# Inverse of the RWKV chunk matrices: the transposed 32x32 blocks by a block transpose on VectorE instead of a third product on TensorE, and the cover pages dealt out anew

## The reference

```python
def step(S, inp):
    r_t, w_t, k_t, v_t, kk_t, a_t = inp
    sa = jnp.einsum('bhij,bhj->bhi', S, -kk_t)
    S = (S * w_t[:, :, None, :]
         + sa[..., None] * (kk_t * a_t)[:, :, None, :]
         + v_t[..., None] * k_t[:, :, None, :])
    y_t = jnp.einsum('bhij,bhj->bhi', S, r_t)
    return S, y_t
```

## Time and profile before

| what | value |
|---|---|
| median of 3 runs | 1367.03 us (1365.85 to 1368.22) |
| the profiled execution, its time | 1366.13 us |
| its span in the trace | 1364.3 us |
| TensorE busy over the span | 1269.6 us (93%) |
| VectorE, ScalarE, GpSimd busy | 811.6, 673.0, 569.9 us |
| chain that ended last | PE 58%, DMA 29%, ACT 5%, DVE 5%, issue 2% |

### The profile page before, as it was taken

The page is one execution under the profiler, slowest core; times in us unless marked ns, Lnnn a source line. Parts: engine busy times, 40 slices in busy tenths (PEclk is TensorE's granted clock), DMA queues, the critical chain, the costliest instruction groups (busy, mean ns, idle before and its releaser), DMA issues.

```text
span 1364.3 us, 22840 instructions
## 1 busy us (share of the span) xinstructions
PE 1269.6 (93%) x8934; PEld 910.7 (67%) x8934; DVE 811.6 (59%) x1854; ACT 673.0 (49%) x1501; POOL 569.9 (42%) x385
## 2 busy tenths in 40 slices
PE   9999999999999999999999988888889888888786
PEld 7988897989999999997896543333434333333232
DVE  5845202464568773457338776666677666667755
ACT  4710233646566665564325564454555444554544
POOL 1100023516878888740005444444434444444342
PEclk9999999999999999999999999999999999999999
DMA  7432322425645556557539999999999999999997
GB/s 265 140 100 90 110 90 75 131 93 171 200 158 188 181 186 200 157 163 267 222 105 414 420 421 422 422 421 421 421 422 422 422 421 421 421 422 422 422 422 302
DMA packets 67940, 381.10 MB, mean 279 GB/s; under 512 B 7552, under 2 KB 7552, under 8 KB 35200
## 3 DMA queue, kind: packets, MB, share of 16 engines
q0 software_dynamic: 37296, 268.45, 47.4%
q1 hardware_dynamic: 29664, 107.84, 24.1%
q10 hardware_dynamic: 880, 3.41, 0.7%
HBM read 378.63 MB, written 1.05 MB: 278 GB/s over the span
## 4 chain that ended last, share of the span: by engine, by line
PE 58%; DMA 29%; ACT 5%; DVE 5%; issue 2%; POOL 0%; SPq 0%; POOLq 0%; DVEq 0%; ACTq 0%
DMA arena_block<-in_experts,arena_block 28%; PE bank L467 23%; PE bank L1111 9%; PE bank L503 5%; PE bank L521 3%; PE bank L465 2%; DVE arena_block L2490 2%; PE bank L1035 2%; PE bank L908 2%; PE bank L485 1%; PE bank L566 1%; DMA const<-in_const 1%; ACT arena_block L1721 1%; PE bank L1135 1%; PE bank L1045 1%
## 5 line engine op out<-in xcount | busy, mean ns | idle before, releaser
L1111 PE MATMUL bank<-arena_block 128*128 128x512 f32 x1012 | 485.4, 610 | 83.4 <-ACT arena_block L1721 81.8
L2627 POOL DMA_INDIRECT arena_block<-in_experts,arena_block x253 | 272.6, 1077 | 467.5 <-PE bank L1111 330.6
L2490 DVE SCALAR_TENSOR_TENSOR arena_block<-arena_block 128x1024 f32<-128x1024 f32 x256 | 314.1, 1227 | 188.5 <-DMA arena_block<-in_experts,arena_block 184.4
L1111 PEld LDWEIGHTS bank<-arena_block 128*128 128x128 f32 x1012 | 178.1, 190 | 350.2 <-ACT arena_block L1721 212.6
L2604 POOL TENSOR_TENSOR w_lo<-ring,w_hi 128x1024 fp32r<-128x1024 f32 x100 | 242.8, 2449 | 85.0 <-ACT w_hi L1219 84.7
L1715 ACT ACTIVATE arena_block<-arena_block 128x1 f32<-128x1 f32 x256 | 75.1, 293 | 278.8 <-DVE arena_block L2490 278.5
L1219 ACT ACTIVATE w_hi<-ring 128x1024 fp32r<-128x1024 f32 x112 | 117.8, 1054 | 51.6 <-PE bank L503 28.8
L467 PE MATMUL bank<-x_hi,w_hi 128*128 128x256 f32 x384 | 109.0, 284 | 0.0
L467 PE MATMUL bank<-x_hi,w_lo 128*128 128x256 f32 x384 | 108.7, 283 | 0.0
L467 PE MATMUL bank<-x_lo,w_hi 128*128 128x256 f32 x384 | 108.7, 283 | 0.0
L1721 ACT ACTIVATE arena_block<-const,arena_block 128x128 f32<-128x128 f32 x256 | 102.7, 401 | 8.3
(11 more groups left out here) (538 smaller groups left out, 2344.6 us busy)
## 6 DMA issues: line engine op xcount, KB each, us to landing
ring<-in_pages SPq DMA_DIRECT2D x175, 512.0 KB, 3.5
wq_pages<-in_pages SPq DMA_DIRECT2D x16, 512.0 KB, 4.4
arena_block<-in_experts,arena_block POOLq DMA_INDIRECT x259, 14.9
arena_block<-in_pages SPq DMA_DIRECT2D x8, 512.0 KB, 7.0
arena_mix<-in_memT ACTq DMA_DIRECT2D x1, 1024.0 KB, 9.0
arena_block<-in_subkT ACTq DMA_DIRECT2D x1, 1024.0 KB, 5.4
const<-in_const SPq DMA_DIRECT2D x1, 974.5 KB, 13.3
out_tok<-arena_block SPq DMA_DIRECT2D x3, 256.0 KB, 7.6
```

What stands on the lines that cost most here:

```text
L1111: last = mm(bank[2 * tt + j][:, :], diag[:, slot, :], uv[slot][:, D + j * 512:D + (j + 1) * 512], start=start, stop=stop)
L2490: stt(uv[s][:, 0:D], uv[s][:, 0:D], 1.0, htok[:, tt, :], ALU.mult, ALU.mult, accum_out=e_act[:, s:s + 1])\
L2627: nc.gpsimd.indirect_dma_start(out=uv[slot], out_offset=None, in_=A["experts"], in_offset=bass.IndirectOffsetOnAxis(ap=eidx[:, n:n + 1], a ...
```

## The change

Inverse no longer makes `dt`. After VectorE has added `dd` to DDn, it makes DTn from DDn by one instruction that transposes each 32x32 block (128x512 elements, 64 blocks). The same is done once ahead of level 0, so that the blocks are made on one side only. TensorE's list of cover pages, and ScalarE's and VectorE's lists beside it, are written anew: with two steps in a level instead of three, Inverse ends three pages sooner in the list, and the four pages of `mv` stand together ahead of the gates.

```diff
         def near_dd(lv):
             pe.wait_ge(S("b_act"), B_ACT[f"pp{lv}"])
             near_product(7, DTn, PPn).then_inc(S("b_pe"), 1)
-
-        def near_dt(lv):
-            near_product(6, PPn, DTn).then_inc(S("b_pe"), 1)
...
-        for side in range(2):
-            if side:
-                a_page(18)
-            for c in range(2):
-                for h in range(8):
-                    j, ft, o = item(c, h)
-                    for b in range(0, P, NEAR):
-                        kb, ab = bT[o:o + 64, ft, c * P + b:c * P + b + NEAR], AR[o:o + 64, ft, c, 0, b:b + NEAR]
-                        at_ = side * T + (4 * c + ft) * NEAR
-                        last = mm(bank[4 + h % 2][b:b + NEAR, at_:at_ + NEAR], *((ab, kb) if side else (kb, ab)), start=True, stop=True)
+        for c in range(2):
+            for h in range(8):
+                j, ft, o = item(c, h)
+                for b in range(0, P, NEAR):
+                    last = mm(bank[4 + h % 2][b:b + NEAR, (4 * c + ft) * NEAR:(4 * c + ft + 1) * NEAR],
+                              bT[o:o + 64, ft, c * P + b:c * P + b + NEAR], AR[o:o + 64, ft, c, 0, b:b + NEAR], start=True, stop=True)
         last.then_inc(S("b_pe"), 1)
+        a_page(18)
...
+        for lv in range(4):
+            a_page(19 + 2 * lv)
             near_pp(lv)
-            pairs(3 * lv)
...
+            pairs(2 * lv)
+            if lv < 3:
+                a_page(20 + 2 * lv)
+            else:
+                pe.wait_ge(S("norm_out"), 1)
+                linear("sbv", hn, by_token=True, part=(0, 1))
             near_dd(lv)
...
+            pairs(2 * lv + 1)
         linear("sbv", hn, by_token=True, part=(1, 1))
...
         def near_add(lv):
             dve.wait_ge(S("b_pe"), B_PE[f"dd{lv}"])
-            dve.wait_ge(S("b_pe"), B_PE[f"dt{lv}"])
-            tt_(DDn, DDn, two(bank[7][:, :], NEAR), ALU.add)
-            tt_(DTn, DTn, two(bank[6][:, :], NEAR), ALU.add).then_inc(S("b_dve"), 1)
+            step(tt_(DDn, DDn, two(bank[7][:, :], NEAR), ALU.add))
+            v.transpose(near_flat(DTn), near_flat(DDn)).then_inc(S("b_dve"), 1)
...
             stt(DTn[:, q::2, :], two(bank[4 + q][:, 0:T], NEAR), -1.0, half8(C_NEAR + NEAR), ALU.mult, ALU.mult)
-            stt(Cn[:, q::2, :], two(bank[4 + q][:, 0:T], NEAR), -1.0, half8(C_NEAR + 2 * NEAR), ALU.mult, ALU.mult)
-            last = stt(DDn[:, q::2, :], two(bank[4 + q][:, T:2 * T], NEAR), -1.0, half8(C_LOW1), ALU.mult, ALU.mult)
+            last = stt(Cn[:, q::2, :], two(bank[4 + q][:, 0:T], NEAR), -1.0, half8(C_NEAR + 2 * NEAR), ALU.mult, ALU.mult)
         done(dve, last, "b_dve", B_DVE["near_read"])
-        tt_(DTn, DTn, level(0), ALU.add)
-        tt_(DDn, DDn, level(0), ALU.add).then_inc(S("b_dve"), 1)
+        step(tt_(DTn, DTn, level(0), ALU.add))
+        v.transpose(near_flat(DDn), near_flat(DTn)).then_inc(S("b_dve"), 1)
```

More of the change, by code:

```diff
@@ L98, in numbered @@
     return {n: i + 1 for i, n in enumerate(names.split())}
-B_PE = numbered("lora_up gate_up kk_sum kk_spread bonus_up vtok near bktok pp0 pairs0 dd0 pairs1 dt0 pairs2 pp1 pairs3 dd1 pairs4 "
-                "dt1 pairs5 pp2 pairs6 dd2 pairs7 dt2 pp3 dd3 dt3 pp32 dd32 pp64 dd64 g0 u0 y0 state g1 u1 y1 gn_mean qk_sum "
+B_PE = numbered("lora_up gate_up kk_sum kk_spread bonus_up vtok near bktok pp0 pairs0 dd0 pairs1 pp1 pairs2 dd1 pairs3 "
+                "pp2 pairs4 dd2 pairs5 pp3 pairs6 dd3 pairs7 pp32 dd32 pp64 dd64 g0 u0 y0 state g1 u1 y1 gn_mean qk_sum "
                 "gn_var sbq_spread gn_spread mk_spread z0 z1 cum0 cum1 sbo score mem_flip mem_out")
@@ L109 @@
 B_DVE = numbered("lora_in kk_mean kk_inv cum_ready fac bonus_in bonus_done scaled near_read near_ready "
-                 "pairs0 pairs1 inv0 pairs2 pairs3 pairs4 inv1 pairs5 pairs6 pairs7 inv2 inv3 dd32 state "
+                 "pairs0 inv0 pairs1 pairs2 inv1 pairs3 pairs4 inv2 pairs5 pairs6 inv3 pairs7 dd32 state "
                  "qk_sq gn_sq qk_mean gn_mean qk_inv gn_inv sbq mk negabs0 ys0 negabs1 soft0 soft1 "
@@ L731, in _ @@
         last.then_inc(S("b_pe"), 1)
-        linear("mk", memn, part=(2, 1))
+        linear("sbv", hn, by_token=True, part=(2, 1))
         pe.wait_ge(S("b_act"), B_ACT["pp32"])
@@ L740, in _ @@
         last.then_inc(S("b_pe"), 1)
-        linear("mk", memn, part=(3, 1))
+        linear("sbv", hn, by_token=True, part=(3, 1))
         pe.wait_ge(S("b_dve"), B_DVE["dd32"])
@@ L746, in _ @@
         last.then_inc(S("b_pe"), 1)
-        linear("mv", memn, by_token=True, part=(0, 1))
+        pe.wait_ge(S("norm_out"), 2)
+        linear("mk", memn, part=(0, 1))
         pe.wait_ge(S("b_act"), B_ACT["pp64"])
@@ L751, in _ @@
         last.then_inc(S("b_pe"), 1)
-        linear("mv", memn, by_token=True, part=(1, 1))
+        linear("mk", memn, part=(1, 1))
         pe.wait_ge(S("b_dve"), B_DVE["pairs7"])
         chunk_g(0)
-        linear("mv", memn, by_token=True, part=(2, 1))
+        linear("mk", memn, part=(2, 1))
         pe.wait_ge(S("b_act"), B_ACT["dd64"])
         chunk_u(0)
-        linear("mv", memn, by_token=True, part=(3, 1))
+        linear("mk", memn, part=(3, 1))
         chunk_y(0)
@@ L765, in _ @@
         last.then_inc(S("b_pe"), 1)
+        linear("mv", memn, by_token=True)
         pe.wait_ge(S("hn_high"), 1)
@@ L1329, in _ @@
         last.then_inc(S("b_act"), 1)
+        a_copy(19)
         for lv in range(4):
-            if lv == 3:
-                take("sbv", flat(sbv), part=(0, 3))
             act.wait_ge(S("b_pe"), B_PE[f"pp{lv}"])
             A_(PPn, two(bank[6][:, :], NEAR), ACT.Copy).then_inc(S("b_act"), 1)
[L1335 to L1346, removed]
+            if lv < 3:
+                a_copy(20 + 2 * lv)
+                a_copy(21 + 2 * lv)
+        take("sbv", flat(sbv), part=(0, 1))
         act.wait_ge(S("b_dve"), B_DVE["inv3"])
@@ L1351, in _ @@
         last.then_inc(S("b_act"), 1)
+        take("sbv", flat(sbv), part=(1, 1))
         act.wait_ge(S("b_pe"), B_PE["pp32"])
@@ L1356, in _ @@
         last.then_inc(S("b_act"), 1)
-        take("mk", mk, part=(2, 1))
+        take("sbv", flat(sbv), part=(2, 1))
         act.wait_ge(S("b_pe"), B_PE["dd32"])
@@ L1362, in _ @@
         last.then_inc(S("b_act"), 1)
-        take("mk", mk, part=(3, 1))
+        take("sbv", flat(sbv), part=(3, 1))
         act.wait_ge(S("b_pe"), B_PE["pp64"])
@@ L1369, in _ @@
         A_(hn_hi, hn, ACT.Copy).then_inc(S("hn_high"), 1)
-        take("mv", flat(mv), part=(0, 1))
+        take("mk", mk, part=(0, 1))
         act.wait_ge(S("b_pe"), B_PE["dd64"])
@@ L1388, in y_copy @@
             A_(Y[:, :, c * P:(c + 1) * P], two(bank[7][:, :], P), ACT.Copy).then_inc(S("b_act"), 1)
-        take("mv", flat(mv), part=(1, 1))
+        take("mk", mk, part=(1, 1))
+        g_copy(0)
+        take("mk", mk, part=(2, 1))
+        u_copy(0)
+        take("mk", mk, part=(3, 1))
+        y_copy(0)
+        take("mv", flat(mv), part=(0, 2))
         high(EARLY[0])
-        g_copy(0)
         take("mv", flat(mv), part=(2, 1))
         high(EARLY[1])
-        u_copy(0)
         take("mv", flat(mv), part=(3, 1))
         high(EARLY[2])
-        y_copy(0)
         take("gate0", gates[:, 0:8, :], ACT.Sigmoid, part=(0, 1))
@@ L1850, in level, with near_flat @@
             return many(cst(C_NEAR + NEAR * lv, NEAR), ITEMS)
+        def near_flat(m):
+            return m.rearrange("p a b -> p (a b)")
         def near_cross(lv):
@@ L1976, in _ @@
         pairs_read(0)
+        near_add(0)
         pairs_read(1)
-        near_add(0)
-        pairs_read(2)
         near_cross(2)
-        pairs_read(3)
         dve.wait_ge(S("in_a_copy"), SPLIT_END - SHIFTED)
         v.memset(DT, 0.0)
+        pairs_read(2)
+        near_add(1)
         norm_apply(1, mem_raw, "mem_g", memn)
+        pairs_read(3)
+        near_cross(3)
         pairs_read(4)
-        near_add(1)
+        near_add(2)
         pairs_read(5)
-        near_cross(3)
+        dve.wait_ge(S("in_a_copy"), N_IN_A - SHIFTED - 4)
+        tt_(sq_of["sbq"], sbq, sbq, ALU.mult)
         pairs_read(6)
+        near_add(3)
+        pairs_read(7)
         dve.wait_ge(S("in_a_copy"), N_IN_A - SHIFTED)
-        tt_(sq_of["sbq"], sbq, sbq, ALU.mult)
-        pairs_read(7)
-        near_add(2)
         tt_(sq_of["sbk"], sbk, sbk, ALU.mult)
         tt_(sq_of["mq"], mq, mq, ALU.mult)
-        near_add(3)
         dve.wait_ge(S("b_dve"), B_DVE["inv3"])
```

23 lines of the change are left out of this document (removed).

## The result

The changed kernel takes 1358.42 us (median of 6 runs, 1357.89 to 1360.91), the kernel before 1367.70 beside it (6 runs, 1365.85 to 1368.93). The ratio is 0.9935, with a 95% interval of 0.9922 to 0.9948: faster by 0.65%. The direction was right, and so was the list of TensorE as the bound; the gain that I forecast was too small.

A forecast was written before the change was run, and what follows sets the result against it. TensorE's gapless list was taken as the bound: 1366.13 - 6.10 (five products) + 0.31 (wait at group 4) = 1360.34 us; with the median 0.90 above, the forecast was 1361.2 us, 0.43% less, range 1358.9 to 1364.0.

The forecast's parts named there:

- What bounds the kernel: From Inverse to the first gate page TensorE works off its list without a gap; removing work shortens it.
- What is removed: Four dt products and the second side of the blocks leave TensorE's list: 5 x 1.22 = 6.10 us.
- Two things I leave at nothing: Two TensorE instruction-stream pauses (0.63 and 0.52 us), chance 0.04 to go too, and the earlier runs' 2.4 us spread.
- the sum: 1366.13 - 6.10 + 0.31 = 1360.34 us for an execution like the profiled one.
- moving them costs nothing by itself: Pages and pairs on TensorE's list keep their number and lengths, 3.65 and 1.06 us, so moving costs nothing.
- What is added: The new VectorE handoff in each level: addition, then transpose; TensorE may go on at 0.91 + X + 0.18 us.
- X: Length of VectorE's 128x512 transpose, taken as 0.69 us; TensorE waits between levels from 3.62 us on.
- The short cover: Group 4 of the pairs, behind the memory's moved norm on VectorE: TensorE waits X - 0.38, 0.31 us, once.
- The covers costed at nothing: Behind Inverse, join copies stay covered by a page; the first gate page has 3.1 us spare: no cost.
- A transpose of some 1.5 us: Rival of a slower, still hidden transpose, X 0.9 to 3.5: cost only at group 4, 1361.5 to 1364.1; chance 0.17.
- Slower than before from X = 4.3: Rival: the transpose becomes the bound, each level waits X - 3.62, gain gone at X = 4.3 us; chance 0.03.

The follow-up runs named there:

- the old cover: Kernel before with the transposes alone, dt and the second side out, cover pages dealt as before: 1359.30 us, ratio 0.9943.
- the dense kernel: Changed kernel with five products that nobody reads put back on TensorE, back to back with others: 1387.17 us, ratio 1.0140.
- the shifted kernel: Kernel before with 32 small matmuls that nobody reads put ahead of the first side of the blocks: 1377.57 us (one run).

## Where the prediction was right and where it failed

**What bounds the kernel.** Right. TensorE's list set the time; what left it came off the time, and the stages behind the stretch moved as a whole (the gathers from 711.3 to 704.4, the last stretch 624.3 us as before).

**What is removed.** The term of 6.10 us was read rightly for its records (1.21 to 1.22 a piece). **What failed is the paragraph "Two things I leave at nothing"**: it left the two pauses of the earlier trace rows out of the sum, gave them a chance of 0.04 to go, and counted only their idle time, 1.15 us, in the lower end of the range. They do not lie beside the change: they stand where TensorE has used up a packet of 256 instructions and the next has only just landed, and with 1280 instructions out of the list both were gone, 1.54 us with their restarts. They are not fixed quantities either: across the runs above a pause was 0.24 to 4.0 us, and the run with the norm moved has one of 0.36 us in the same list of TensorE. So the 1.54 us hold for this pair of executions. A second step failed too, "moving them costs nothing by itself": the joints gave 0.95 us. By the trace a removed product was worth 1.6 us, pauses and joints included (8.21 over five with the old cover), and not 1.22. The sign was to be had beforehand: both pauses of the earlier trace rows stand inside products of 32x32, and none in a page.

**What is added.** Right: X was bounded from 0.35 to 3.5 and taken at 0.69 for the row with the same tile, and is 0.71. The estimate of 1.24 us from the Trainium skill ("VectorE: DVE Perf Modes", section on the three transpose paths, for 16-bit values) is not what this shape takes. The addition over the same tile gave the price.

**The short cover.** Right place, 0.14 us for 0.31, by the signal gaps.

**The covers costed at nothing.** Right: the gate page is ready 3.0 us early (3.1 forecast), and no join waits.

**The rivals.** A transpose of some 1.5 us would hardly have mattered: with X at 1.46 the median was 1360.23. Slower than before from X = 4.3: a straight line between the stretches with four and with seven transposes meets the 114.25 of before at X = 4.1, an estimate. It comes near only because two errors are opposed: the gain that has to be eaten up is 8.45 us and not 6.10, and the waits of 2.31 and 3.18 us cost more than their length.

**The numbers.** For the profiled execution the sum gave 1360.34 and 1359.11 was measured, with the half clock at 237 us in it; without those 1.5 us it would be 1357.6, 2.7 us under the sum: 1.54 pauses, 0.95 joints, 0.17 at group 4. The medians differ by 9.3 us, 0.8 more than the stretch. Runs of one kernel spread by 3 us, in part by pauses and falls of the clock that come in some executions, so I assign that remainder to nothing.

**What stays open.** Why a given packet comes late. The changed kernel and the one with the norm moved have the same list on TensorE, and yet only one of the two profiled executions has a pause. Whether the page loads in the same stretch delay a packet was not tried. Why a page takes 3.51 to 3.60 us in some places of the list and 3.65 in others is not shown. Nor is it known why the clock fell at 237 us in this execution of after, and not in that of before.

## What to carry to other kernels

Price a run of tiny matmuls by its instructions as well as by its records: here 64 matmuls of 32x32 were 256 instructions, one packet of 16 KB, used up in 1.22 us, and each such product that left the list was worth some 1.6 us. A pause "<-issue" inside such a group is a sign that the stream is at its limit there: it may go when the group thins, as it did here, and more than the records' time is to be expected when work of that kind is added. For an operation that the trace lacks, the row with the same tile in and out was the right price. A wait of TensorE can cost more than its length: those of 2.31 and 3.18 us did here, those of 0.81 and 1.3 did not.

## What the runs showed of the hardware

- VectorE transposes the 32x32 blocks of a 128x512 tile of 4-byte values in 0.71 us, next to 0.69 for an addition of that size.
- Long idle times of TensorE were followed by a granted clock of 0.50 (1.2 GHz): behind the wait of 2.31 us for VectorE and behind pauses of the stream alike. In the dense kernel, behind the pause of 3.09 us, the windows read

```profile
95.00:98.30 3.30, 0.78 (x93) 0.69 (x82) 0.00 (x0) 0.00 (x0) 0.00 (x0) 1.00 0.40 145
98.30:105.00 6.70, 6.13 (x51) 4.61 (x51) 2.82 (x6) 0.00 (x0) 0.00 (x0) 0.50 0.01 2
105.00:107.00 2.00, 2.00 (x13) 1.43 (x13) 0.00 (x0) 0.00 (x0) 0.00 (x0) 0.96 0.00 0
```

  and in the shifted kernel it was 0.52 from 83.5 to 87.0, behind the pause of 2.11, and 0.50 from 162.2 to 165.6, behind that of 1.78. In the stretch, idle times of 1.3 us and less had no such window behind them.
- The half clock also came with TensorE busy ahead of it. In the run with the norm moved, one such window lies ahead of everything that the edit touches:

```profile
54.00:56.50 2.50, 2.50 (x14) 1.99 (x15) 2.46 (x5) 0.69 (x1) 0.00 (x0) 1.00 0.60 206
56.50:60.00 3.50, 3.50 (x19) 3.50 (x19) 3.31 (x6) 3.50 (x5) 0.00 (x0) 0.51 0.01 4
```

  The profiles of before and of after have 1.00 at the same place of the program. The window at 237 us of after has its like in five of the other eleven profiled executions, each 52.6 to 53.4 us behind the first gate page and with TensorE busy ahead of it; the other six have none there. So a difference of 1.5 us between two profiles of this kernel may be no difference of the kernels.
